# The large activation buffers and the small tables change places in SBUF in a two-model float32 kernel

## The reference

```python
def hybrid_layer(h, p_i, positions, norm_g, w_in, b_f, qk_g, w_out, w_ple, ple_norm_g, w_ple_gate):
    z = rms_norm(h, norm_g) @ w_in                      # 1024 -> 4104
    # 8 heads of forgetting attention, 8 heads of dilated attention, each head 64 wide
    h = h + jnp.concatenate([oa, ob], axis=-1) @ w_out
    gate = jax.nn.sigmoid(rms_norm(h, ple_norm_g) @ w_ple_gate)
    return h + (p_i @ w_ple) * gate

def second_block(x, mem, ...):
    for l in range(DEPTH):
        x = x + 0.5 * swiglu(rmsnorm(x, ffn1_norm[l]), ffn1_w1[l], ffn1_w3[l], ffn1_w2[l])   # 1024 -> 2816 -> 1024
        proj = rmsnorm(x, mix_norm[l]) @ w_in[l]
        # HGRN2 recurrence on one half, pooling over 2/4/8/16 frames on the other
        x = x + jnp.concatenate([o_a, o_b], axis=-1) @ w_out[l]
        x = x + mem_cross_attention(rmsnorm(x, xa_norm[l]), rmsnorm(mem, mem_norm[l]), xa_wq[l], xa_wkv[l], xa_wo[l])
        x = x + 0.5 * swiglu(rmsnorm(x, ffn2_norm[l]), ffn2_w1[l], ffn2_w3[l], ffn2_w2[l])
    return rmsnorm(x, final_norm)
```

## Time and profile before

| what | value |
|---|---|
| median of 3 runs | 3251.05 us (3232.97 to 3259.46) |
| the profiled execution, its own time | 3251.05 us |
| its span, from the first to the last instruction | 3249.3 us |
| TensorE (PE) busy | 3126.7 us, 96% of the span, 14562 matmuls |
| VectorE (DVE) busy | 1647.1 us, 51% |
| ScalarE (ACT) busy | 1104.6 us, 34% |
| GpSimd (POOL) busy | 67.2 us, 2% |
| mean share of the 16 DMA engines busy | 24.0% |

### The profile page before, as it was taken

One profiled execution on the slowest core, in us unless ns is written; L12 is line 12 of the kernel. 1 busy time (PEld: TensorE's weight loads), 2 busy tenths in 40 slices (PEclk: granted clock), 3 DMA queues, 4 the chain that ended last, 5 costly groups with the idle time before them and its releaser, 6 DMA issues.

```text
span 3249.3 us, 33980 instructions
## 1 busy us (share of the span) xinstructions
PE 3126.7 (96%) x14562; PEld 2588.9 (80%) x14562; DVE 1647.1 (51%) x1870; ACT 1104.6 (34%) x1310; POOL 67.2 (2%) x70
## 2 busy tenths in 40 slices
PE   7999999999999999989999999999999889999998
PEld 6787888778888887877878888788888778688886
DVE  4445554455554546455445454644565454454545
ACT  4435443344432225423432222322235333432222
POOL 0000000000000000020000000000000110000000
PEclk8999999899999999989999999999999799999999
DMA  3111222011233222202312222222232003232321
GB/s 120 65 41 51 76 87 74 30 67 46 91 104 113 96 99 104 82 10 91 130 65 91 102 93 91 94 101 91 100 110 101 27 29 128 77 104 91 104 91 65
DMA packets 41495, 270.58 MB, mean 83 GB/s; under 512 B 5728, under 2 KB 5984, under 8 KB 9984
## 3 DMA queue, kind: packets, MB, share of 16 engines
q1 hardware_dynamic: 41344, 268.40, 24.0%
HBM read 266.22 MB, written 2.10 MB: 83 GB/s over the span
## 4 chain that ended last, share of the span: by engine, by line
PE 80%; DVE 10%; ACT 7%; issue 1%; DVEq 1%; DMA 0%; SPq 0%; ACTq 0%
PE PS L216 23%; PE PS L218 22%; PE PS L217 22%; DVE w_lo L201 4%; ACT w_hi L193 3%; PE PS L848 2%; PE PS L1575 2%; PE PS L514 2%; DVE XT L1067 2%; PE PS L837 1%; DVE total L280 1%; PE PS L1824 1%; PE PS L1799 1%; PE PS L486 1%; DVEq L1491 1%
## 5 line engine op out<-in xcount | busy, mean ns | idle before, releaser
L193 ACT ACTIVATE w_hi<-w_raw 128x2048 fp32r<-128x2048 f32 x242 | 463.4, 1915 | 1251.8 <-PE PS L218 1248.2
L201 DVE TENSOR_TENSOR w_lo<-w_raw,w_hi 128x2048 fp32r<-128x2048 f32 x242 | 554.6, 2292 | 435.1 <-ACT w_hi L193 434.4
L216 PE MATMUL PS<-uh_b,w_hi 128*128 128x512 f32 x1312 | 511.7, 390 | 0.0
L218 PE MATMUL PS<-uh_b,w_lo 128*128 128x512 f32 x1312 | 510.5, 389 | 0.0
L217 PE MATMUL PS<-ul_b,w_hi 128*128 128x512 f32 x1312 | 510.5, 389 | 0.0
L216 PE MATMUL PS<-w_hi,uh_a 128*128 128x512 f32 x768 | 311.0, 405 | 27.1 <-DVE ul_a L271 10.7
L216 PE MATMUL PS<-uh_a,w_hi 128*128 128x512 f32 x800 | 313.6, 392 | 8.1 <-DVE ul_a L481 6.2
L218 PE MATMUL PS<-uh_a,w_lo 128*128 128x512 f32 x800 | 311.9, 390 | 0.0
L217 PE MATMUL PS<-ul_a,w_hi 128*128 128x512 f32 x800 | 311.9, 390 | 0.0
L217 PE MATMUL PS<-w_lo,uh_a 128*128 128x512 f32 x768 | 306.1, 399 | 0.0
L218 PE MATMUL PS<-w_hi,ul_a 128*128 128x512 f32 x768 | 305.6, 398 | 0.0
(11 more groups left out here) (287 smaller groups left out, 3948.1 us busy)
## 6 DMA issues: line engine op xcount, KB each, us to landing
w_raw<-in_weights SPq DMA_DIRECT2D x242, 1024.0 KB, 4.9
XT<-in_xT SPq DMA_DIRECT2D x8, 256.0 KB, 8.9
mem_raw<-in_mem SPq DMA_DIRECT2D x2, 1024.0 KB, 4.8
out<-XT SPq DMA_DIRECT2D x8, 256.0 KB, 2.2
bands<-in_bands SPq DMA_DIRECT2D x2, 768.0 KB, 6.3
mask_numbers<-in_masks SPq DMA_DIRECT2D x1, 1152.0 KB, 7.2
p_raw<-in_pT SPq DMA_DIRECT2D x2, 512.0 KB, 3.5
lb<-in_lb_logits SPq DMA_DIRECT2D x2, 512.0 KB, 5.8
```

The costliest lines, as they stand in the source:

```text
L193: act.activation(self.hi[g % 2][:], self.raw[g % 2][:], ACT.Copy).then_inc(self.hi_done.sem, 1)
L201: dve.tensor_tensor(self.lo[g % 2][:], self.raw[g % 2][:], self.hi[g % 2][:], ALU.subtract).then_inc(self.lo_done.sem, 1)
L216: pe.matmul(out, sh, mh, start=first, stop=False)
L218: return pe.matmul(out, sl, mh, start=False, stop=last)
```

## The change

No instruction is added, removed or moved: on each of the five engines the listing of the changed kernel's instructions, waits included, has the same rows in the same order, and differs from the other in the line numbers of a few start and end rows alone. What changes is where tensors lie in SBUF. The 88 KB gap above the weight buffers is gone: `ident`, the norms' buffers and the small tensors of both models come down into its place, and the large buffers follow above the first model's small tensors. `first_memory` hands back the address `ub` of `uh_b`, and `second_memory` puts its large tensors at the same `ub`, with `mix2` 16 KB below it.

```diff
-def first_memory(mem, k, big):
+def first_memory(mem, k):
...
     m.ang, m.turns, m.red, m.over = (mem.put(n, [P, NT, HALF]) for n in ("ang", "turns", "red", "over"))
-    mem.top = big
     m.mix = mem.put("mix1", [P, NT, D])
     at = mem.top
...
-    assert mem.top <= big + 88 * 1024
-    return m
-
-
-def second_memory(mem, k, big, ua, rows_at):
+    return m, at
+
+
+def second_memory(mem, k, ub, ua, rows_at):
     m = Box()
-    ub = big + 16 * 1024
...
-    mem.top = at = big
+    assert mem.top <= ub - 16 * 1024
+    mem.top = ub - 16 * 1024
+    at = mem.top
     m.mix = mem.put("mix2", [P, NT, D])
...
-    big = mem.top
-    mem.top = big + 88 * 1024
     ident = mem.put("ident", [P, P])
...
-    m1 = first_memory(mem, k, big)
+    m1, ub = first_memory(mem, k)
     mem.top = free
-    m2 = second_memory(mem, k, big, ua, rows_at)
+    m2 = second_memory(mem, k, ub, ua, rows_at)
```

## The result

The changed kernel is slower: its median is 3270.61 us (3260.76 to 3277.03, 20 runs) against 3242.71 us (3232.79 to 3259.46, 20 runs) for the kernel before. The ratio is 1.0079, with a 95% interval of 1.0066 to 1.0091. With more runs the median of the kernel before also came 8 us under the 3251.05 of the three runs shown. So the time did move: the interval leaves out 1, though the loss stays under the 1% that the forecast called no change, and the time lies inside the stated range.

A forecast was written before the change was run, and what follows sets the result against it. TensorE, busy 96% of the span, was taken as the bound, with VectorE and ScalarE in short stages between large products. The sum was 3251.05 + 0 + 0 + 0 + 0 = 3251 us, range 3223 to 3280 us.

The forecast's parts named there:

- the matmul term: Matmuls streaming moved tensors (`uh_b`, `ul_b`, `ff_h_hi`, `ff_h_lo`): taken as 0, bounds -6 to +42 us.
- equal windows: Two feed-forward stages, on `uh_a` and `uh_b`, each have 291 matmuls of line 216 in 200 us at clock 1.00.
- the count of 6048: Matmuls said to stream a moved tensor: 3936 on `uh_b` and `ul_b`, 2112 on `ff_h_hi` and `ff_h_lo`.
- The first rival: TensorE's reads of moved buffers meet VectorE's and ScalarE's accesses, slowing matmuls: 3251 + 42 = 3293 us; chance 4%.
- The threshold: Slower matmuls on moved buffers decide from 32.5 us / 6048 = 5.4 ns per matmul on.
- Instructions and order: Instructions, order and waits: none added, removed or moved, so no stall goes or comes; 0 us.
- VectorE and ScalarE: Five 128x512 groups at different addresses: place matters at most 3 ns of 685, 1.4 us either way; taken as 0.
- the erratic groups: VectorE's widely varying `PT` copy, masked copy into `AT` and product on `E`: -9.7 to +65.7 us, taken as 0.
- the second rival: Three widely varying VectorE groups depend on place and go to their long times: 3317 us, halfway 3284; chance 3%.
- Transfers: Weight blocks and `XT` keep their addresses, small tensors move; from all of 6.5 us less to 0, taken as 0.
- the third rival: Large buffers on a multiple of 256 bytes make transfers and reads faster: 23.6 us less, 3227 us; chance 5%.
- The clock: Granted clock 0.92 in window 0 to 325, 1.00 in 1950 to 2275; drops should stay, but for run-to-run differences.

The follow-up runs named there:

- e5: The changed kernel with the split weights `w_hi` and `w_lo` 128 bytes higher against `uh_a`, `w_raw` and the large buffers; 3263.77 us, ratio 1.0068.
- e3: The kernel before with all tensors 128 bytes higher, so all distances stay as before; 3242.75 us, ratio 1.0007.
- e4: The changed kernel with all tensors 128 bytes higher; 3267.32 us, ratio 1.0086.

## Why the prediction was wrong

**The step that failed is the matmul term**, "I take 0"; it measured 28 us. The prediction compared `uh_a` with `uh_b` in the trace before, found 390 and 389 ns, and concluded that place does not matter. Both stood at distance 0 from the split weights, as every streamed tensor did; so the comparison varied the address by 98304 bytes and the quantity that counts not at all. The address table of the change had the answer's ingredient, 23680 = 92 x 256 + 128, and I used it only to ask about a tensor's own place, on VectorE and for transfers. The second argument, equal windows, had the same blind spot, and so had `mem_R` on a multiple of 256: VectorE reads it, and no weights are loaded beside it.

**The term's measured size.** With the 96 matmuls on `p_hi` and `p_lo`, which the count of 6048 left out, 6144 matmuls gained 5 to 6 ns. Their groups' busy times rose by 8.0, 7.9 and 7.9 us on `uh_b` and `ul_b`, by 3.4, 3.6 and 3.6 us on `ff_h_hi` and `ff_h_lo` and by 0.6 on `p_hi` and `p_lo`: 35 us. One wait gave some back. The view of waits has, before and after,

```profile
PEld PS L216 <- DVE XT L1067: 22.0, 43, 0.5
PEld PS L216 <- DVE XT L1067: 16.3, 43, 0.4
```

so 5.7 us of the slower matmuls fall into 43 waits for VectorE's addition to `XT`, and 35 - 6 = 29 us are left. The starts say the same: from start to start these 6144 matmuls take 1421.3 us in the trace before and 1449.3 after, 28.0 us more, where the medians differ by 27.9 and the ratio of 1.0079 gives 26 us. The spans of the two profiled executions differ by only 17.8 us; their mean granted clocks are 0.965 and 0.968, so TensorE was at 1.2 GHz for 2 x 0.035 x 3249 = 227 us before and 2 x 0.032 x 3267 = 209 us after. The trace after thus had 18 us less at half the clock, which spares it about 9 us if TensorE was at work in them; 17.8 + 9 = 27 agrees with the medians.

**What was luck.** The time, 3270.61 us, fell into the range and the loss stayed under 1% with a wrong mechanism. The matmuls' 35 us are more than the 32.5 us that 1% of the time is; that the loss ended below 1% is due to the wait, which the prediction did not have. And the median of the kernel before came 8 us under the 3251.05 us that the sum started from, which hid part of the 28 us in the distance between forecast and result.

**The first rival** had the right engine and the right sign, and its bound of 7 ns a matmul, 42 us, held the measured 6 ns; it was given 4%. Its cause was wrong. It blamed VectorE and ScalarE, whose groups of the earlier trace rows changed by at most 3 ns and beside which the matmuls are no slower than without them; the pair that e5 shows are the two tensors that TensorE itself reads. The rule of the Trainium skill's page "SBUF — State Buffer", section "Who interferes with whom", that I set beside it, that TensorE does not wait for another engine at SBUF, is not contradicted by these runs: the 6 ns are there with the other engines idle. It was no reason against a cost inside TensorE, and I let it weigh as if it were. The threshold did not hold: above 5.4 ns per matmul I had put a loss of over 1%, and 5 to 6 ns made 0.8%, since the wait gave 5.7 us back.

**What was right.** Instructions and order: unchanged; of the waits, the one above shrank. VectorE and ScalarE: the groups of the earlier trace rows came back within 3 ns (`R` 597 to 600 is the largest), and the erratic groups of the earlier trace rows to within 1 ns of their old medians and 3 ns of their shortest and longest times, so the second rival falls, and the product on `E` still is long where GpSimd works. Transfers: the waits on a DMA are 3.8 and 3.1 us where they were 3.6 and 2.9, so the third rival's gain from alignment did not appear, and nothing on the chain waited for a transfer. The clock: the window 0 to 325 has 0.93 against 0.92, 1950 to 2275 has 0.99 against 1.00, close to before but not the same, and the 18 us of lower clock between the two traces are within what executions of one program show: the mean clocks of the changed kernel's runs lie between 0.966 and 0.971, which is 0.005 x 2 x 3267 = 33 us.

**What stays open.** Why the distance counts, and why 64 is nearly free and 192 is not, is not shown by these runs. That the weight load must run at the same time as the stream (the PEld rows above overlap the matmul) is argued from the roles in e5 and not shown; a run that streams without loading was not made. Nor was it tried whether the 256-column products escape for their length or for another reason.

## What to carry to other kernels

When a change moves tensors in SBUF, look at the distances between the tensors that one engine reads at the same time, not only at their own alignment: in these 512-column split products the streamed tensor and the one loaded as weights were fastest a multiple of 256 bytes apart, slices included, and a 64-byte rounding of allocations does not keep that. A comparison inside one trace proves nothing about a quantity that is the same in all its rows; write down first what each candidate cause would have to differ in. In a kernel that is 96% TensorE, 6 ns on 6144 matmuls is a measurable change with no instruction touched, and the matmul groups by tensor show it directly.

## What the runs showed that I had not expected

Matmuls that stream 512 columns of these float32 pairs go from a mean of 389 to 395 or 396 ns in the profile (from 226.8 to 232.7 ns from start to start, 229.1 to 233.9 in the windows) when the streamed and the loaded tensor are 32, 128, 160, 192 or 224 bytes off a multiple of 256 from each other, to 391 to 393 at 64 and to 394 to 399 at 96. The cost did not follow either tensor's own address (e3, e4), is the same whichever of the two is streamed (e5), did not appear with 256 columns (283 ns either way), is there with all other compute engines idle, and comes without any wait in the trace: only the durations and the distances between starts show it.
